# Attention: exponentials turned by products with diagonal matrices of the reciprocal sums, in place of scaling them and transposing

## The chip, the cores and the metric

The kernel runs on one core of a Trainium2 chip. The metric is the device time of one execution in microseconds (us); the median of the runs of the kernel before is 1780.18 us. Five engines work side by side, each with its own list of instructions, and meet through semaphores: PE (TensorE, matrix products; PEld is its loading of weights), DVE (VectorE), ACT (ScalarE), POOL (GpSimd) and SP (which issues the DMAs of this kernel).

## The reference, cut to what matters

The network is a block with gated linear attention and an MLP, then a block with a gated delta rule, a sparse attention and an MLP, on 512 tokens of width 1024 in float32. The change is in the sparse attention, whose last lines are

```python
s = jnp.einsum('bqcgd,bqncd->bqcgn', qg, k_g).astype(jnp.float32) * scale
s = jnp.where(valid[:, :, None, None, :], s, -jnp.inf)
p = jax.nn.softmax(s, axis=-1).astype(v_g.dtype)
o = jnp.einsum('bqcgn,bqncd->bqcgd', p, v_g)
```

There are 8 query heads, 2 key heads, and head size 128. The softmax needs, for each query, the exponentials of its scores divided by their sum.

## The kernel before, in words

The attention (lines 1371 to 1497) works through 8 steps, i = 0 to 7, one query head each, with e = i % 2 the key head and the parity of most buffers. A step handles all 512 queries in 4 tiles q of 128; tile q has P * (q + 1) keys, so the scores of a head are 128 x 1280 numbers, kept in `ms[e]` with queries on partitions. In the order of the data, a step is:

- `queries` (L1446, DVE) scales the head's queries; `turn` (L1131, PE) multiplies them by a swap matrix; `pool_rope` (L1136, POOL) and `dve_rope` (L1142 and L1145, DVE) make the rotated queries `aq`.
- `scores` on PE (L1395) makes 4 products of 512, 384, 256 and 128 columns.
- `scores` on DVE (L1461) adds the mask, takes the maximum and writes `ms[e]`; L1466 scales the maxima.
- ACT takes the exponential in place (L1433) with the sums in `r_sum`.
- DVE inverts the sums (L1471) and scales the 4 tiles of `ms[e]` in place (L1475), one `tensor_scalar` each.
- PE transposes the 10 blocks of 128 x 128 that are on or below the diagonal into PSUM (L1409), in the order of `K_ORDER`; the counter `pt_ps` rises three times in a step.
- ACT copies them to `p_t` (L1438, four copies). PE multiplies them with the values (L1416, four products, 1280 columns in all). DVE multiplies by the gate (L1454).

The engines run these in an order written by hand (`body`). In body i, PE does the scores of step i + 1, the transposes of step i, the products with the values of step i, then `turn` of step i + 2. DVE does the reciprocal and the scaling of step i, the masks of step i + 1, `queries` of step i + 2, `output` of step i, then the rope of step i + 2. ACT does the exponentials and the copies of step i. The last body has no work ahead in it. Each engine takes its list strictly in that order. After the attention a fence lets all engines meet, and the gated delta rule follows.

Of the kernel before, what the change touches and what calls it, by code (L numbers as in the profile page):

```python
# [19 lines left out]
ALU = mybir.AluOpType  # L20
# [3 lines left out]
P = 128  # L24
SEQ, D, DFF = 512, 1024, 4096
KT = D // P
TT = SEQ // P
# [72 lines left out]
def build(nc, t, out, const_square, const_wide, gb_rows):  # L100
    with ExitStack() as ctx:
        def sb(name, shape, dt=F32):
            return ctx.enter_context(nc.sbuf_tensor(name, shape, dt))
# [4 lines left out]
        s = {}  # L108
# [19 lines left out]
        ident = sb("ident", [P, P])  # L128
# [10 lines left out]
        def take(*shape):  # L139

            n = int(np.prod(shape))
            v = arena[:, at[0]:at[0] + n]
            at[0] += n
            assert at[0] <= 22400, at[0]
            if len(shape) == 2:
                v = v.rearrange("p (a b) -> p a b", a=shape[0])
            if len(shape) == 3:
                v = v.rearrange("p (a b c) -> p a b c", a=shape[0], b=shape[1])
            return v
# [4 lines left out]
        def tiles(ap, n=TT):  # L154
            return ap.rearrange("p (t c) -> p t c", t=n)
# [902 lines left out]
        ms = [None, ci_si_keep[:, 0:1280]]  # L1058
# [16 lines left out]
        n_max, r_sum = take(2 * TT), take(TT)  # L1075
# [4 lines left out]
        av = take(2, SEQ)  # L1080
        gtmp = take(3, SEQ)
        lg = gtmp[:, 0:2]
        top8 = take(3, 8)
        assert at[0] <= kept0, (at[0], kept0)
        off = [0, 128, 384, 768]
# [41 lines left out]
        def pe_rope(pe, c, src, swap):  # L1127

            if not (isinstance(c, int) and c == 0):
                pe.wait_ge(s["rp_ss"], c)  # L1130
            pe.matmul(b[5][:], swap[:], src, start=True, stop=True).then_inc(s["rp_ps"], 1)  # L1131
# [6 lines left out]
        def dve_rope(dve, c, src, sin):  # L1138
            if not (isinstance(c, int) and c == 0):
                dve.wait_ge(s["rp_out"], c)  # L1140
            dve.wait_ge(s["rp_ps"], c + 1)
            dve.tensor_tensor(rp_s, b[5][:], sin, ALU.mult).then_inc(s["rp_ss"], 1)  # L1142
            dve.wait_ge(s["rp_cc"], c + 1)
            dve.wait_ge(s["rp_ss"], c + 1)
            dve.tensor_tensor(src, rp_c, rp_s, ALU.add).then_inc(s["rp_out"], 1)  # L1145
# [226 lines left out]
        S_ORDER = (3, 1, 0, 2)  # L1372
# [4 lines left out]
        def att_steps(eng, body):  # L1377

            with eng.Fori(0, HPK - 1) as j:
                body(j, 0, 2)  # L1380
                body(j, 1, 2)
            body(HPK - 1, 0, 1)
            body(HPK - 1, 1, 0)

        def pe_att(pe):
            def turn(i, e):

                pe.wait_ge(s["r_y"], i + 3)
                pe_rope(pe, i + 7, aq[:, e], swap_a)

            def scores(i, e):
                pe.wait_ge(s["rp_out"], i + 8)
                for q in S_ORDER:
                    bk, o = s_at[q]
                    last = pe.matmul(bk[:, o:o + P * (q + 1)], aq[:, e, q * P:(q + 1) * P], ak[:, e, 0:P * (q + 1)],  # L1395
                                     start=True, stop=True)
                    if q != 0:
                        last.then_inc(s["s_ps"], 1)

            def body(j, e, ahead):  # L1400
                i = 2 * j + e
                if ahead >= 1:
                    pe.wait_ge(s["nm_r"], TT * i + TT)
                    scores(i + 1, 1 - e)
                pe.wait_ge(s["pn_r"], TT * i + TT)
                for k in K_ORDER:
                    bk, o = t_at[k]
                    for q in range(k, TT):
                        last = pe.transpose(bk[:, o + (q - k) * P:o + (q - k + 1) * P],  # L1409
                                            ms[e][:, off[q] + k * P:off[q] + (k + 1) * P], ident[:])  # L1410
                    if k != 3:
                        last.then_inc(s["pt_ps"], 1)
                pe.wait_ge(s["att_done"], i + 1)
                for n, k in enumerate(K_ORDER):
                    pe.wait_ge(s["pt_sb"], TT * i + n + 1)
                    last = pe.matmul(b[4][:, k * P:SEQ], v_key[e][:, k, :], p_t[:, koff[k]:koff[k] + SEQ - k * P],  # L1416
                                     start=(n == 0), stop=(n == TT - 1), skip_group_check=True)
                last.then_inc(s["pv_ps"], 1)
                if ahead >= 2:
                    turn(i + 2, e)  # L1420

            turn(0, 0)
            scores(0, 0)
            turn(1, 1)
            att_steps(pe, body)

        def act_att(act):
# [14 lines left out]
        def dve_att(dve):  # L1442
            def queries(j, e):
                i, h = 2 * j + e, j + HPK * e
                dve.wait_ge(s["r_r"], h + 3)
                dve.scalar_tensor_tensor(aq[:, e], q_all[:, bass.ds(h, 1)].rearrange("p a t -> p (a t)"),  # L1446
                                         gains[:, G_QN:G_QN + 1], q_sq[:, bass.ds(h, 1)].rearrange("p a t -> p (a t)"),
                                         ALU.mult, ALU.mult).then_inc(s["r_y"], 1)

            def output(j, e):  # L1450
                i, h = 2 * j + e, j + HPK * e
                dve.wait_ge(s["pv_ps"], i + 1)
                o = o_att[:, bass.ds(h, 1)].rearrange("p a t -> p (a t)")
                dve.scalar_tensor_tensor(o, o, 1.0, b[4][:], ALU.add, ALU.mult).then_inc(s["att_done"], 1)  # L1454

            def scores(i, e):
                for n, q in enumerate(S_ORDER):
                    dve.wait_ge(s["s_ps"], (TT - 1) * i + (1, 2, 3, 3)[n])
                    w = P * (q + 1)
                    bk, o = s_at[q]  # L1460
                    dve.tensor_tensor_reduce(out=ms[e][:, off[q]:off[q] + w], in0=bk[:, o:o + w], in1=sel[:, off[q]:off[q] + w],  # L1461
                                             scale=1.0, scalar=NOT_CAUSAL, op0=ALU.add, op1=ALU.max,
                                             accum_out=n_max[:, 4 * e + q:4 * e + q + 1]).then_inc(s["nm_r"], 1)
                dve.wait_ge(s["nm_r"], TT * i + TT)
                nm = n_max[:, 4 * e:4 * e + 4]
                dve.tensor_scalar(nm, nm, -P ** -0.5, None, ALU.mult).then_inc(s["nms"], 1)  # L1466

            def body(j, e, ahead):
                i = 2 * j + e
                dve.wait_ge(s["ex_a"], TT * i + TT)  # L1470
                dve.reciprocal(r_sum, r_sum).then_inc(s["rs_r"], 1)  # L1471
                dve.wait_ge(s["rs_r"], i + 1)
                for q in S_ORDER:
                    m = ms[e][:, off[q]:off[q] + P * (q + 1)]
                    dve.tensor_scalar(m, m, r_sum[:, q:q + 1], None, ALU.mult).then_inc(s["pn_r"], 1)  # L1475
                if ahead >= 1:
                    scores(i + 1, 1 - e)
                if ahead >= 2:
                    queries(j + 1, e)
                output(j, e)  # L1480
                if ahead >= 2:
                    dve_rope(dve, i + 9, aq[:, e], sa)

            queries(0, 0)
            dve_rope(dve, 7, aq[:, 0], sa)
            queries(0, 1)
            scores(0, 0)
            dve_rope(dve, 8, aq[:, 1], sa)
            for i in range(ATT_H):
                body(i // 2, i % 2, min(2, ATT_H - 1 - i))  # L1490
# [739 lines left out]
```

## Time and profile before

| | us |
|---|---|
| median of 3 runs | 1780.18 |
| lowest, highest | 1779.96, 1781.19 |
| the profiled execution | 1785.38 |
| its span in the trace | 1783.6 |
| of which the attention, from its first `queries` to its last `output` | 872.8 to 948.9 |

The profiled execution took 5.2 us more than the median of the runs without a profiler, and 1.8 us of it lie outside the span. The trace tells where in the span each engine was busy (us from the span's start), what an idle engine waited for, and, in the chain, which piece of work released the next one, back from the end. The granted clock of TensorE is given as a share of full speed (2.4 GHz); 0.50 is the lower of its two levels.

### The profile page before, as it was taken

Reading aid. Unit: us, or ns where it says so; the run is one execution under the profiler, and the core shown is the slowest. Engines: PE = TensorE matmul, PEld = TensorE weight load, DVE = VectorE, ACT = ScalarE, POOL = GpSimd, SP = SyncE. Lnnn points to the kernel's source line nnn. Section 1 sums busy time; section 2 is a strip of 40 time slices with the busy share of each in tenths; the row PEclk is TensorE's granted clock in tenths of the full one; section 3 lists DMA queues with packets and bytes.
Section 4 is the critical chain, followed back from the end, with each engine's and each line's share of the span. In section 5 each row is a group of like instructions: output and inputs, shape, how many; then the busy total and the mean of one; then the engine's idle time right before and its main releaser. Section 6 shows DMA issues by size and latency. Waiting matters only on the chain.

```text
span 1783.6 us, 24801 instructions
## 1 busy us (share of the span) xinstructions
PE 1659.3 (93%) x9418; PEld 1316.4 (74%) x9418; DVE 984.9 (55%) x1489; ACT 680.3 (38%) x1033; POOL 241.9 (14%) x220
## 2 busy tenths in 40 slices
PE   6899968999999987899879898998989899999999
PEld 4677757888888864567547786877878688888887
DVE  5455545444454455378775757566674544444453
ACT  6355543313132334223444535254443332313232
POOL 0134330000000030134210311304022000000000
PEclk7999979999999997899999999999999999999999
DMA  4222202333333332223102213121220233333333
GB/s 136 72 60 72 71 13 82 95 96 93 105 94 94 94 87 73 59 60 83 50 0 83 60 49 83 39 70 49 72 70 15 82 86 103 94 95 94 106 93 96
DMA packets 258157, 135.06 MB, mean 76 GB/s; under 512 B 10699, under 2 KB 254940, under 8 KB 258068
## 3 DMA queue, kind: packets, MB, share of 16 engines
q1 hardware_dynamic: 258068, 133.84, 26.6%
q8 instruction: 61, 1.00, 0.2%
q14 instruction: 28, 0.23, 0.0%
HBM read 131.64 MB, written 2.18 MB: 75 GB/s over the span
## 4 chain that ended last, share of the span: by engine, by line
PE 70%; DVE 11%; issue 10%; ACT 6%; POOL 3%; DMA 0%; DVEq 0%; POOLq 0%; PEldq 0%; ACTq 0%; SPq 0%; PEld 0%
PE bank L229 17%; PE bank L230 17%; PE bank L231 17%; PE bank L1574 3%; DVE arena L1880 3%; PE bank L491 2%; DVE w_lo L213 2%; ACT w_hi L209 2%; PE bank L493 1%; PE bank L492 1%; PE bank L1395 1%; PE bank L1416 1%; PE bank L1131 1%; PE bank L1590 1%; PE bank L1627 1%
## 5 line engine op out<-in xcount | busy, mean ns | idle before, releaser
L229 PE MATMUL bank<-h_hi,w_hi 128*128 128x512 f32 x984 | 401.7, 408 | 38.4 <-DVEq L1899 13.7
L230 PE MATMUL bank<-h_lo,w_hi 128*128 128x512 f32 x984 | 391.3, 398 | 0.0
L231 PE MATMUL bank<-h_hi,w_lo 128*128 128x512 f32 x984 | 390.9, 397 | 0.0
L213 DVE TENSOR_TENSOR w_lo<-raw,w_hi 128x1024 fp32r<-128x1024 f32 x218 | 281.2, 1290 | 141.3 <-ACT w_hi L209 139.4
L209 ACT CAST w_hi<-raw 128x1024 fp32r<-128x1024 f32 x234 | 245.1, 1047 | 254.5 <-PE bank L231 243.1
L229 PEld LDWEIGHTS bank<-h_hi,w_hi 128*128 128x128 f32 x984 | 189.8, 193 | 97.0 <-issue 36.7
L229 PE MATMUL bank<-m_hi,w_hi 128*128 128x512 f32 x608 | 238.7, 393 | 6.4 <-DVE w_lo L213 6.2
L231 PE MATMUL bank<-m_hi,w_lo 128*128 128x512 f32 x608 | 237.3, 390 | 0.0
L230 PE MATMUL bank<-m_lo,w_hi 128*128 128x512 f32 x608 | 237.2, 390 | 0.0
L230 PEld LDWEIGHTS bank<-h_lo,w_hi 128*128 128x128 f32 x984 | 190.6, 194 | 41.3 <-issue 3.2
L231 PEld LDWEIGHTS bank<-h_hi,w_lo 128*128 128x128 f32 x984 | 189.7, 193 | 41.0
L229 PEld LDWEIGHTS bank<-m_hi,w_hi 128*128 128x128 f32 x608 | 114.4, 188 | 33.2 <-issue 6.5
L231 PEld LDWEIGHTS bank<-m_hi,w_lo 128*128 128x128 f32 x608 | 114.5, 188 | 24.1
L230 PEld LDWEIGHTS bank<-m_lo,w_hi 128*128 128x128 f32 x608 | 114.6, 188 | 23.4
L948 DVE TENSOR_TENSOR arena<-bank,arena 128x512 f32<-128x512 f32 x64 | 44.3, 692 | 147.0 <-PE bank L231 147.0
L938 DVE TENSOR_TENSOR arena<-arena 128x512 f32<-128x512 f32 x64 | 44.3, 693 | 133.4 <-ACT arena L914 133.4
L491 PE MATMUL bank<-h_hi,w_hi 128*128 128x512 f32 x248 | 106.2, 428 | 0.0
L914 ACT ACTIVATE arena<-bank 128x512 f32<-128x512 f32 x64 | 38.3, 598 | 175.4 <-PE bank L231 175.4
L493 PE MATMUL bank<-h_hi,w_lo 128*128 128x512 f32 x248 | 97.2, 392 | 0.0
L492 PE MATMUL bank<-h_lo,w_hi 128*128 128x512 f32 x248 | 96.9, 391 | 0.0
L1574 PE MATMUL bank<-arena 64*64 64x64 f32 x1984 | 73.0, 220 | 7.1 <-DVE arena L2022 4.0
L1574 PEld LDWEIGHTS bank<-arena 64*64 64x64 f32 x1984 | 67.2, 134 | 13.2 <-issue 10.5
(273 smaller groups left out, 2027.9 us busy)
## 6 DMA issues: line engine op xcount, KB each, us to landing
raw<-in_l_w_ff SPq DMA_DIRECT2D x64, 512.0 KB, 4.0
raw<-in_w_in SPq DMA_DIRECT2D x64, 512.0 KB, 3.8
raw<-in_w_mlp_up SPq DMA_DIRECT2D x32, 512.0 KB, 4.0
raw<-in_w_mlp_down SPq DMA_DIRECT2D x32, 512.0 KB, 3.7
raw<-in_l_w_in SPq DMA_DIRECT2D x24, 512.0 KB, 3.8
raw<-in_l_w_out SPq DMA_DIRECT2D x8, 512.0 KB, 3.7
arena<-gb_rows SPq DMA_DIRECT2D x16, 256.0 KB, 4.6
raw<-in_w_out SPq DMA_DIRECT2D x8, 512.0 KB, 3.7
```

Of the source, the lines that this page charges most:

```text
L209: act.copy(w_hi[q.par][:], raw[q.par][:]).then_inc(s["w_hi_ready"], 1)
L213: dve.tensor_tensor(w_lo[q.par][:], raw[q.par][:], w_hi[q.par][:].bitcast(F32), ALU.subtract).then_inc(s["w_ready"], 1)
L229: pe.matmul(g_bank[q.par][:], w_hi[q.par][:, k], hi[:, k], start=(k == 0), stop=False)
L230: pe.matmul(g_bank[q.par][:], w_hi[q.par][:, k], lo[:, k], start=False, stop=False)
L231: last = pe.matmul(g_bank[q.par][:], w_lo[q.par][:, k], hi[:, k], start=False, stop=(k == KT - 1))
L491: pe.matmul(g_bank[q.par][:], w_hi[q.par][:, k], hi[:, k], start=(k == 0), stop=False)
L492: pe.matmul(g_bank[q.par][:], w_hi[q.par][:, k], lo[:, k], start=False, stop=False)
L493: last = pe.matmul(g_bank[q.par][:], w_lo[q.par][:, k], hi[:, k], start=False, stop=(k == KT - 1))
L938: dve.tensor_tensor(sq[:, u % 2], rl[:, u % 2], rl[:, u % 2], ALU.mult).then_inc(s["sqr"], 1)
L948: dve.tensor_tensor(down[:, u % 2], g_bank[q.par][:], r_sqr, ALU.mult).then_inc(s["dn"], 1)
L1574: return pe.matmul(o, left, right, start=True, stop=True, skip_group_check=True)
L1880: dve.scalar_tensor_tensor(y, ub[:, jj:jj + SEQ], w, y, ALU.mult, ALU.add).then_inc(s["c_chain"] if jj < CONV - 1 else s["c_y"], 1)
```

## The change

The scaling of the 4 tiles of exponentials is gone. Instead DVE makes `r_dg`, four 128 x 128 diagonal matrices with the reciprocal sums of the four tiles of queries on their diagonals, in one `tensor_tensor`, in a part of the arena that nothing used. PE then multiplies each 128 x 128 block of unscaled exponentials with the diagonal matrix of its tile of queries, as an ordinary float32 `matmul`, where it transposed the block with the identity before. The product of a block's transpose with the diagonal matrix is the scaled and transposed block. Since `r_dg` is a single buffer, DVE waits before it writes it until the products of the step before have read it.

```diff
+        r_dg = tiles(gtmp[:, 2])
...
-                pe.wait_ge(s["pn_r"], TT * i + TT)
+                pe.wait_ge(s["pn_r"], i + 1)
                 for k in K_ORDER:
                     bk, o = t_at[k]
                     for q in range(k, TT):
-                        last = pe.transpose(bk[:, o + (q - k) * P:o + (q - k + 1) * P],
-                                            ms[e][:, off[q] + k * P:off[q] + (k + 1) * P], ident[:])
+                        last = pe.matmul(bk[:, o + (q - k) * P:o + (q - k + 1) * P],
+                                         ms[e][:, off[q] + k * P:off[q] + (k + 1) * P], r_dg[:, q], start=True, stop=True)
...
                 dve.reciprocal(r_sum, r_sum).then_inc(s["rs_r"], 1)
                 dve.wait_ge(s["rs_r"], i + 1)
-                for q in S_ORDER:
-                    m = ms[e][:, off[q]:off[q] + P * (q + 1)]
-                    dve.tensor_scalar(m, m, r_sum[:, q:q + 1], None, ALU.mult).then_inc(s["pn_r"], 1)
+                if i:
+                    dve.wait_ge(s["pt_ps"], (TT - 1) * i)
+                dve.tensor_tensor(r_dg, ident[:].unsqueeze(1).broadcast_to([P, TT, P]),
+                                  r_sum.unsqueeze(2).broadcast_to([P, TT, P]), ALU.mult).then_inc(s["pn_r"], 1)
```

## Rows read from the trace of the kernel before

**Rows 1.** Chain of work, 868 to 955 us, one step: start us, us, what

```profile
892.38 2.43 PE bank L1395 x8
894.81 1.09 PE bank L1409 x10
895.90 0.02 issue
895.92 2.43 PE bank L1416 x8
898.35 0.87 PE bank L1131 x2
...
899.31 0.70 DVE arena L1142
...
900.11 0.70 DVE arena L1145
```

**Rows 2.** Timeline, steps 2 and 6: start, us, engine, line, operation, idle time before and releaser

```profile
900.86 2.43 PE L1395 MATMUL bank<-arena 128*128 128x512 f32 x8 [1.65 <-DVE arena L1145]
900.92 1.27 DVE L1475 TENSOR_SCALAR arena<-arena 128x512 f32<-128x512 f32 x4
...
903.12 1.26 PE L1409 MATMUL bank<-ident,arena 128*128 128x128 f32 x10
...
903.75 1.42 ACT L1438 COPY arena<-bank 128x512 f32<-128x512 f32 x4 [4.89 <-PE bank L1409]
...
904.39 0.30 PEld L1416 LDWEIGHTS bank<-arena 128*128 128x128 f32 x2 [0.26 <-ACT arena L1438]
...
937.06 1.26 PE L1409 MATMUL bank<-ident,arena 128*128 128x128 f32 x10
...
941.07 0.21 ACT L1433 ACTIVATION_READ_ACCUMULATOR arena<-arena 128x1 f32 x1
```

**Rows 3.** Waits of the stretch 868 to 955 us: total us, times, longest us

```profile
PE bank L1409 <- DVE arena L1475: 2.2, 1, 2.2
```

**Rows 4.** Groups by line and shape, 872 to 951 us: count, busy us, mean ns

```profile
L1409 PE MATMUL bank<-ident,arena 128*128 128x128 f32 x80 | 11.1, 290 | 2.2 <-DVE arena L1475 2.2
...
L1145 DVE TENSOR_TENSOR arena<-arena 128x512 f32<-128x512 f32 x8 | 5.5, 692 | 0.8
...
L1438 ACT COPY arena<-bank 128x512 f32<-128x512 f32 x8 | 4.7, 586 | 34.7 <-PE bank L1409 34.7
```

**Rows 5.** Chain, 1000 to 1013 us: 16 products with 128 columns, in one run

```profile
1008.70 3.57 PE bank L1590 x32
```

**Rows 6.** Groups by line and shape of DVE, whole span

```profile
L1932 DVE TENSOR_TENSOR arena<-arena 128x512 f32<-128x512 f32 x8 | 9.8, 1227 | 0.0
```

**Rows 7.** Chain of the last step, 936 to 949 us

```profile
938.43 2.41 PE bank L1416 x8
...
940.86 0.69 DVE arena L1454
941.55 0.10 DVE arena L1471
...
941.67 1.29 DVE arena L1475 x4
...
943.01 2.31 PE bank L1409 x10
945.32 2.85 PE bank L1416 x8
```

**Rows 8.** Stretches of PE: us, length, busy (instructions), granted clock, DMA share, GB/s

```profile
942.00:943.00 1.00, 0.00 (x0) 1.00 0.00 0
943.00:944.00 1.00, 0.99 (x5) 0.57 0.00 0
...
945.00:946.00 1.00, 1.00 (x4) 0.50 0.00 0
946.00:947.00 1.00, 1.00 (x4) 0.72 0.00 0
```

**Rows 9.** Other idle times of PE and the clock in and after them

```profile
247.70:249.60 1.90, 0.08 (x1) 1.00 0.00 0
249.60:251.00 1.40, 1.34 (x9) 0.73 0.05 12
```

**Rows 10.** The same for steady steps of the attention (all engines)

```profile
892.00:901.00 9.00, 6.95 (x29) 4.24 (x30) 6.48 (x21) 3.58 (x12) 1.27 (x1) 1.00 0.00 0
901.00:910.00 9.00, 7.33 (x30) 4.38 (x31) 6.51 (x20) 3.58 (x12) 1.27 (x1) 1.00 0.00 0
```

## The prediction

> **What bounds the kernel now.** I read the chain of waits first, cut to the attention. A step of it repeats every 8.47 us, and PE carries most of it [rows 1]: the scores of the next head (2.43 us), the ten transposes (1.09), the products with the values (2.43), the product that turns the next queries (0.87); then PE stands still for 1.65 us while DVE does the two halves of the rope, and it begins again [rows 1, 2]. The reader should see what is not in this chain: neither the scaling L1475 nor the copies L1438.
>
> Then I read the timeline of step 2. The scaling runs from 900.92 to 902.19, while PE is at the scores that it began at 900.86; PE turns to the transposes at 903.12 [rows 2]. DVE is done 0.93 us before it is asked. The waits say the same for all steps: the transposes waited for the scaling once only, for 2.2 us [rows 3], and that is the last step, where no scores of a next head stand in between [rows 7]. So in seven of eight steps the work that the change takes from DVE is free, and what it adds to PE is on the path.
>
> One more thing is in the timeline. Ten transposes should need 1.09 us, but from the first of them to the first product with the values 1.27 us pass: this product waited for the first copy of ACT, which began at 903.75 and takes 0.586 us for its largest piece [rows 2, 4]. So 0.18 us of a step belong to ACT, under which longer PE work can hide.
>
> **The change, part by part.**
>
> *Transposes become products.* A transpose is one instruction of 128 columns: 80 for 8 steps of 10 [rows 4], 0.109 us apart (1.09 over 10) [rows 1]. The trace has no product with a diagonal matrix, but it has float32 products of the same size, 128 x 128 with 128 columns and new weights each time: L1590 issues 16 in a run, they show as 32 instructions, and the run takes 3.57 us, 0.112 us an instruction [rows 5]. The scores tell the same: 4 products, 8 instructions [rows 1]. So a product costs two instructions of about the same time as one transpose, 0.223 us. Ten take 2.23 us.
>
> After that the first copy is no longer late: its four blocks are 8 of the 20 instructions, done after 0.90 us; the copy begins some 0.19 us behind them (as now: four transposes are 0.44 us, and it begins 0.63 us after the first of them), takes 0.59 us, and is through at 1.7 us, before 2.23 [rows 2, 4]. A step therefore grows from 1.27 to 2.23 us between the first block and the first product with the values: +0.96 us. In step 6 the distance now is 1.37 (937.06 to 938.43) [rows 2, 7], so +0.86. Seven steps: 6 x 0.96 + 0.86 = **+6.6 us**. Bounds: if the wait of 0.18 us for a copy stays, +0.18 each, +7.9 in all; if the products go at 0.109 us as the transposes do, -0.06 each, +6.2. I take 0.112, the row of the same shape.
>
> *Scaling becomes one multiplication on DVE.* Four instructions, 1.27 us [rows 2], go; one `tensor_tensor` of 128 x 512 float32 from SBUF comes. L1145 is the same shape at 0.692 us [rows 4]; the highest row of this shape is L1932 at 1.227 us [rows 6]. The operands here are read with repeats, which no row of L1145 has; I take 0.69 and keep 1.23 as the upper end. At either, DVE stays ahead of PE in steps 0 to 6, so the worth is nothing; even at 1.27 us it was 0.93 early. What starts earlier behind it on DVE are the masks L1461, and these wait for PE's scores. In the last step it is on the path: 1.29 - 0.69 = **-0.6 us** [rows 7] (bounds -0.1 to -0.6). From this I take 0.1 back: the last two copies of step 6 now end later than they do, since the products end later, and with them the last exponentials, which are in ACT's queue behind these copies. They end at 941.28 now, 0.27 us before the reciprocal begins [rows 2, 7], and would end about level with it. That leaves **-0.5 us**.
>
> *The new wait of DVE on `pt_ps`.* Behind it are the multiplication, the masks of the next head, `queries`, `output` and the rope, so a late answer would be dear. It is never late: on PE the products of step i - 1 come before the products with the values of step i - 1, and DVE has waited for those in `output` of step i - 1 already. Cost: the 0.02 to 0.04 us of a wait that is met, beside work of PE. Nothing on the path.
>
> *TensorE's clock in the last step.* Now PE stands still from 940.84 to 943.01, 2.17 us [rows 7], and as it starts again its granted clock falls from 1.00 to 0.57 and 0.50, that is to 1.2 GHz, until about 946.3 [rows 8]. Transposes and products take 2.31 + 2.85 = 5.16 us there [rows 7], where the transposes and products of a steady step have 1.09 + 2.43 = 3.52 [rows 1]. With the change the stop is 2.17 - 0.5 = 1.7 us. The steps before show such stops seven times between 882 and 935, of 1.65 us (the last of them 1.74), with the clock at 1.00 throughout (one stop stands in [rows 2], two of the stretches with their clock in [rows 10]); after a stop of 1.9 us at 247.7 it fell [rows 9]. 1.7 is nearer to 1.65. I take it that the clock stays: 2.23 + 2.43 = 4.66 in place of 5.16, **-0.5 us**. If it falls as now, for 3.3 us at half speed, 1.65 us are lost: 6.31 in place of 5.16, +1.15.
>
> *The sum.* +6.6 - 0.5 - 0.5 = **+5.6 us**, and everything behind the fence shifts by it: the profiled execution would go from 1785.38 to 1791.0, its span from 1783.6 to 1789.2. That execution is 5.2 us over the median; the difference is the profiler's and I carry it over. Forecast for the median: 1780.18 + 5.6 = **1785.8 us**. Its own range, from 0.109 us an instruction (-0.4) to the wait for the copy that stays (+1.3) and a multiplication of 1.23 us (+0.5): 1785.2 to 1787.6, and about 0.6 us either way for how the runs differ.
>
> **The rivals.**
>
> *The clock falls in the last step all the same.* All as above, but +1.15 in place of -0.5: +7.3 us, **1787.5**. For it speaks that stops of 1.7 and 1.9 us are near each other, and that the products will be at another place in time. Against it: seven stops of 1.65 to 1.74 us without a fall.
>
> *A product is one instruction, as a transpose is (the other side).* If a product with a diagonal matrix went through at the price of a transpose, 10 x 0.112 = 1.12 us, the copy would stay the later of the two, seven steps would not change, and the last step would gain: -0.5 for the shorter work on DVE, and 1.12 + 0.18 + 2.43 = 3.73 in place of 5.16. Together -1.9 us, **1778.3**: not slower. It decides for the change as soon as ten blocks take less than about 1.4 us. Against it: every float32 product that I looked at has two instructions [rows 1, 5].
>
> *DVE's work is on the path in every step.* If PE's stop of 1.65 us hung on how early DVE gets to the rope, the 0.6 us saved would come back seven times: 5.6 - 4.2 = +1.4 us, **1781.6**, no difference that can be measured. Against it: before the rope DVE waits for PE's turned queries, not the reverse, and before the transposes it is 0.93 us early.
>
> *A product costs four times a transpose.* Then ten take 40 x 0.109 = 4.36 us, a step grows by 3.1, and with the last step (4.36 + 2.43 for 5.16, and -0.5) the sum is 7 x 3.1 + 1.1 = +22.8 us, **1803**. Against it are the 32 instructions for 16 products [rows 5].
>
> The Trainium skill, "TensorE: Matmul & The Clock Gate", section Terms, says that the transpose mode is 4x faster for FP32, which speaks against this change and would give that last time. The trace doesn't bear it out: it has a factor of two, 0.223 us to 0.109.
>
> **How the numbers follow.** Forecast 0.62; the clock falls 0.18; one instruction a product 0.06; DVE on the path 0.05; four times 0.03; something that I don't see 0.06, split evenly between small drifts on both sides. The range is 1784.0 to 1788.8: it takes in the forecast with its bounds, the fallen clock with the wait for the copy that may stay, and leaves out the last three rivals. A measurement of this kernel can tell about 0.2% (3.6 us) from no change, so the border of slower is 1783.7 and that of faster 1776.6. Slower: 0.62 + 0.18 + 0.03 and most of what I don't see, 0.88. Same: 0.06 + 0.05 and a little less for what could go further, 0.10. Faster: 0.02.
>
> **What would show it.** In the trace of the changed kernel: 160 instructions at L1409's place, 0.112 us apart, and 2.23 us from the first of them to the first product with the values; the load of weights of that product no longer waits for a copy; a period of 9.43 us a step with the same stop of 1.65 before the scores; the new multiplication at 0.69 us, over 1 us before PE asks for it, and its wait on the counter without idle time; in the last step a stop of some 1.7 us, the clock at 1.00 after it. Wrong would be: a stop before the scores that is not 1.65, 80 or 320 instructions, or time that moved outside the stretch 873 to 955.

## The result

The changed kernel takes 1785.66 us at the median of 20 runs, the kernel before 1780.49 us at the median of 20. The ratio is 1.0026, with a 95% interval of 1.0018 to 1.0033: slower by 4.6 us (3.2 to 5.9); the medians as they stand differ by 5.2. The forecast was 1785.8 us.

The profile agrees where the change is. From the first `queries` of the attention to the end of its last `output`, called the stretch from here on, the kernel before took 76.1 us (872.76 to 948.88), the changed one takes 81.0 us (868.03 to 949.06): +4.9 us. The spans as wholes, 1783.6 and 1784.4 us, do not show this; the last experiment shows why. Each run has one trace, so what is said of the clock in a step is said of that one execution.

One step in the chain of waits of the changed kernel (start us, us, what; in it L1396 is the scores, L1410 the products that turn the blocks, L1417 the products with the values, L1132 the product for the queries):

```profile
897.80 2.43 PE bank L1396 x8
900.23 2.23 PE bank L1410 x20
902.46 2.16 PE bank L1417 x8
904.62 0.87 PE bank L1132 x2
...
905.59 0.70 DVE arena L1143
...
906.38 0.70 DVE arena L1146
```

Against [rows 1], 10 transposes in 1.09 us have become 20 instructions in 2.23 us, and the products with the values went from 2.43 to 2.16 us. The period of a step went from 8.47 to 9.33 us. The timeline of the same step shows why L1417 is shorter than L1416 was. First the row of the kernel before that follows the last one of step 2 in [rows 2], its load of weights for the second product, then the changed kernel:

```profile
904.93 0.19 PEld L1416 LDWEIGHTS bank<-arena 128*128 128x128 f32 x1 [0.24 <-ACT arena L1438]
```

```profile
900.06 2.39 PE L1410 MATMUL bank<-arena 128*128 128x128 f32 x20
...
901.15 0.86 ACT L1439 COPY arena<-bank 128x512 f32<-128x512 f32 x2 [5.16 <-PE bank L1410]
...
902.19 0.30 PEld L1417 LDWEIGHTS bank<-arena 128*128 128x128 f32 x2
902.29 2.32 PE L1417 MATMUL bank<-arena 128*128 128x512 f32 x8
902.73 0.19 PEld L1417 LDWEIGHTS bank<-arena 128*128 128x128 f32 x1 [0.24 <-issue]
```

Before, the first load waited 0.26 us for a copy of ACT [rows 2] and began together with its product, and the load for the second product waited for the next copy and began 0.54 us after the first. Here neither waits for ACT: the first begins 0.10 us ahead of its product, the one for the second product 0.44 us after that product. From the first block to the first product with the values it is 2.23 us (900.06 to 902.29).

The last step, in the chain, and the clock in it (the stretch, its length, PE busy, granted clock, DMA share, GB/s):

```profile
942.02 0.69 DVE arena L1455
...
942.92 0.70 DVE arena L1476
943.63 0.04 issue
943.67 2.50 PE bank L1410 x20
946.17 2.17 PE bank L1417 x8
```

```profile
942.00:943.00 1.00, 0.00 (x0) 1.00 0.00 0
943.00:944.00 1.00, 0.33 (x3) 1.00 0.00 0
944.00:945.00 1.00, 1.00 (x11) 1.00 0.00 0
945.00:946.00 1.00, 1.00 (x11) 1.00 0.00 0
```

PE stood still for 1.7 us (in [rows 7] 2.2), the clock stayed at 1.00 (in [rows 8] it fell), and the two groups took 4.67 us where they took 5.16.

### The profile page after: what moved, and what is told of

It reads as the page before. It is cut to its first block, busy times and chain, and to the rows that moved or that the text cites. A ratio compares the mean times of both kernels' runs of the same rounds, so it can differ in the third digit from the quotient of the medians.

```text
span 1784.4 us, 24944 instructions
## 1 busy us (share of the span) xinstructions
PE 1660.0 (93%) x9498; PEld 1321.1 (74%) x9498; DVE 980.8 (55%) x1465; ACT 681.3 (38%) x1033; POOL 241.8 (14%) x220
## 4 chain that ended last, share of the span: by engine, by line
PE 71%; DVE 11%; issue 9%; ACT 6%; POOL 2%; DMA 0%; DVEq 0%; POOLq 0%; PEldq 0%; ACTq 0%; SPq 0%; PEld 0%
PE bank L229 17%; PE bank L231 17%; PE bank L230 17%; PE bank L1576 3%; DVE arena L1882 3%; PE bank L491 2%; DVE w_lo L213 2%; ACT w_hi L209 2%; PE bank L493 2%; PE bank L492 2%; PE bank L1396 1%; PE bank L1410 1%; PE bank L1417 1%; PE bank L1132 1%; PE bank L1592 1%
```

## The experiments

Each comes from one of the two kernels by the edit shown. The stretch is read from its trace as above; the ratio is to the kernel before.

| run | step, us | stretch, us | median, us | ratio, 95% interval |
|---|---|---|---|---|
| before | 8.47 | 76.1 | 1780.49 | |
| after | 9.33 | 81.0 | 1785.66 | 1.0026, 1.0018 to 1.0033 |
| products with the identity | 9.33 | 83.4 | 1788.76 | 1.0037, 1.0023 to 1.0051 |
| transposes, no scaling | 8.47 | 74.1 | 1776.55 | 0.9976, 0.9966 to 0.9985 |
| transposes twice | 9.28 | 83.0 | 1787.63 | 1.0035, 1.0021 to 1.0049 |
| stop filled | 8.47 | 74.8 | 1776.42 | 0.9974, 0.9963 to 0.9986 |
| last multiplication longer | 9.33 | 83.3 | 1789.78 | 1.0053, 1.0033 to 1.0073 |
| the others longer | 9.33 | 81.5 | 1782.46 | 1.0013, 1.0001 to 1.0025 |
| before, other order | 7.96 | 72.8 | 1777.80 | 0.9985, 0.9975 to 0.9994 |
| after, other order | 7.41 | 69.5 | 1773.50 | 0.9966, 0.9952 to 0.9980 |
| before, queries first too | 6.51 | 64.5 | 1765.92 | 0.9914, 0.9899 to 0.9929 |
| after, queries first too | 7.41 | 69.6 | 1772.51 | 0.9954, 0.9941 to 0.9968 |
| before, both and the fill | 6.51 | 62.9 | 1767.80 | 0.9925, 0.9911 to 0.9938 |
| before again | 8.47 | 76.1 | 1780.99 | 0.9999, 0.9990 to 1.0008 |

**The two parts alone.** First the products without the shorter work on DVE:

```diff
-                        last = pe.transpose(bk[...], ms[e][...], ident[:])
+                        last = pe.matmul(bk[...], ms[e][...], ident[:], start=True, stop=True)
```

> One part alone: the blocks are turned by float32 products with the identity, the scaling on DVE stays as before. The stretch from the first queries to the last output of the attention was 76.1 us before and 81.0 after the change. Theory (PE's instructions set the step, DVE's scaling is hidden in seven of eight steps): steps of 9.33 us as after the change, a stop of about 2.2 us before the last products as before it, so the clock falls there (1.65 us more): stretch 83.3 us. Rival (what DVE does sets the step): the stretch stays near 76 us. If the clock held in spite of the stop: 81.7 us.

Measured: steps of 9.33 us and a stretch of 83.4 us. Then the shorter work on DVE with the transposes, from the changed kernel:

```diff
-                        last = pe.matmul(bk[...], ms[e][...], r_dg[:, q], start=True, stop=True)
+                        last = pe.transpose(bk[...], ms[e][...], ident[:])
```

> The other part alone: DVE makes the diagonal matrices in place of scaling, PE transposes with the identity as before. The kernel leaves out the division by the sums in the attention. Theory: steps of 8.47 us as before (the shorter DVE work brings nothing in them), in the last step a stop of 1.6 us in place of 2.2 and the clock at full speed after it: stretch 74.1 us against 76.1. Rival (DVE on the path in every step): 0.6 us less in each of seven steps, about 70 us. If the clock falls in the last step all the same: 75.5 us.

Measured: steps of 8.47 us and 74.1 us. So the products cost their 0.86 us in every step, and DVE's part is worth nothing in the steps but 2.0 us at the end, of which 0.6 us is its own shorter work and 1.3 us the clock: transposes and products take 3.83 us there, from 937.78 to 941.61 in the second fence below, where they took 5.16. Both came out as the theory had them. The two do not add up to the change (+7.3 - 2.0 = +5.3 against +4.9), mostly since the products alone lose more to the clock: 6.32 us where the changed kernel takes 4.67 without a fall, 1.65 us against 1.33. The last steps of the two, in the chain, first the products with the identity, then the transposes:

```profile
944.07 1.29 DVE arena L1475 x4
...
945.40 3.68 PE bank L1409 x20
949.08 2.64 PE bank L1416 x8
```

```profile
937.03 0.70 DVE arena L1476
...
937.78 1.31 PE bank L1410 x10
939.20 2.41 PE bank L1417 x8
```

**Is it the number of instructions?**

```diff
+                        for _ in range(2):
                             last = pe.transpose(bk[...], ms[e][...], ident[:])
```

> The kernel before, with every block transposed twice into the same place: as many PE instructions in a step (20) as the products have, none of them a product. Theory (the number of 128-column instructions is the price): 20 x 0.109 us = 2.18, steps of 9.3 us, in the last step the clock falls as before: stretch 82.7 us. Rival (a float32 product has a price beyond its two instructions, in its weight loads for one): steps clearly shorter than the 9.33 us of the changed kernel.

Measured: steps of 9.28 us, 0.05 less than with products, which is 20 instructions at 0.109 in place of 0.112. One step and the last one in the chain:

```profile
928.67 2.18 PE bank L1410 x20
930.86 2.16 PE bank L1417 x8
...
944.63 3.27 PE bank L1410 x20
947.90 2.99 PE bank L1417 x8
```

A float32 product of 128 columns costs what its two instructions cost. And here too L1417 takes 2.16 us and not 2.43: whatever work stands between the first block and the products with the values, ACT's copies get their time from it.

**The clock in the last step.** Two products of 512 columns that nothing reads fill PE's stop in the kernel before:

```diff
                 last.then_inc(s["pv_ps"], 1)
+                if ahead == 1:
+                    pe.wait_ge(s["nm_r"], TT * ATT_H)
+                    for _ in range(2):
+                        pe.matmul(b[0][:], aq[:, e, 0:P], ak[:, e, :], start=True, stop=True)
```

> The kernel before, with two more products of 512 columns (four instructions, some 0.9 us) that nothing reads, on PE in its stop of 2.2 us ahead of the last step's transposes; the stop that is left is 1.3 us. Theory (the length of the stop makes the clock fall): the clock stays at 1.00, the last transposes and products take 3.7 us in place of 5.16, stretch 74.6 us against 76.1. Rival (it falls for where in time it stands, or since transposes follow): no change, 76.1 us.

Measured: 74.8 us. The timeline of PE, with the fill in the second line, and the clock after it:

```profile
932.33 2.40 PE L1416 MATMUL bank<-arena 128*128 128x512 f32 x8
934.56 1.88 PE L1422 MATMUL bank<-arena 128*128 128x512 f32 x4
936.91 1.31 PE L1409 MATMUL bank<-ident,arena 128*128 128x128 f32 x10 [0.46 <-DVE arena L1479]
```

```profile
937.00:938.00 1.00, 1.00 (x10) 1.00 0.00 0
```

The fill took about 1.9 us and left a stop of 0.5 us, not the 1.3 expected (1.88 us for four instructions where I had counted 0.9), and the clock stayed. The reverse, in the changed kernel:

```diff
+                for n in range(1 if i == ATT_H - 1 else 0):
+                    dve.tensor_tensor(tiles(sc[:, SEQ * n:SEQ * (n + 1)]), ident[:]..., r_sum..., ALU.mult)
                 dve.tensor_tensor(r_dg, ident[:]..., r_sum..., ALU.mult).then_inc(s["pn_r"], 1)
```

> The changed kernel, with one more multiplication of the same shape (0.69 us, into a buffer that nothing reads) ahead of the one of the last step alone. The stop of PE before the last products becomes 1.68 + 0.69 = 2.37 us. Theory (a stop above some 1.9 us lets the clock fall): stretch 81.0 + 0.69 + 1.65 = 83.4 us. Rival (the products, unlike transposes, keep or at once regain the clock): 81.7 us.

Measured: 83.3 us; the stop was 2.3 us, and the clock fell although the work after it was products:

```profile
948.00:949.00 1.00, 0.47 (x4) 1.00 0.00 0
949.00:950.00 1.00, 1.00 (x9) 0.71 0.00 0
950.00:951.00 1.00, 1.00 (x7) 0.50 0.00 0
```

Here the clock fell 0.9 us after PE had begun again, in the kernel before after 0.1 us. So in the last step the clock follows the stop, in both kernels: seven traces have a stop of 0.5 to 1.7 us there and keep the clock, seven have one of 2.2 to 2.3 us and lose it. The fill is also work, and both edits move the time at which PE begins again, so the length is not shown to act alone. It doesn't decide elsewhere. All 14 traces have the code ahead of the attention in common, with a stop of 1.89 us near 250 us (the one of [rows 9]) and one of 2.34 us near 80 us. After the first the clock fell in 3 traces, after the second in 7. The kernel before against itself, which comes last below, has after its stop of 1.89 us

```profile
248.40:249.80 1.40, 1.36 (x12) 1.00 0.05 12
```

where [rows 9] has 0.73, and after the stop of 2.34 us the kernel with the filled stop and the one with the products with the identity have

```profile
81.50:84.50 3.00, 2.98 (x17) 1.00 0.00 0
81.70:84.70 3.00, 3.00 (x14) 0.70 0.00 0
```

What a fall costs in the last step is seen against the same work without one: 1.3 us for the transposes (5.16 against 3.83), 1.6 to 1.7 us for the products (6.32 and 6.31 against 4.67). The doubled transposes have no such partner. Against a steady step they lose as much as the products with the identity (6.26 against 4.34, 6.32 against 4.39), and in both the lower level lasted 3.4 us. The Trainium skill, "TensorE: Matmul & The Clock Gate", section Part 4: PE-mode transpose, says that transposes do not count as activity for the clock as products do; these runs give no sign of it. They are no test of it either, since in each the products with the values follow before the clock is back.

**How much DVE has to spare.**

```diff
+                for n in range(2 if i < ATT_H - 1 else 0):
+                    dve.tensor_tensor(tiles(sc[:, SEQ * n:SEQ * (n + 1)]), ident[:]..., r_sum..., ALU.mult)
```

> The changed kernel, with two more multiplications of the same shape (1.38 us of DVE, into buffers that nothing reads) in each step but the last. Theory (DVE has about 1.5 us to spare before PE asks for the diagonal matrices): steps of 9.33 us as without them, stretch 81.0 us. Rival (DVE on the path in every step): 1.38 us more in each of seven steps, 90.7 us.

Measured: steps of 9.33 us but for the first, which went to 9.78; 81.5 us. In the first step the scores of the head before had run at the lower clock and the exponentials were late, so DVE had less to spare there and PE waited. In the others 1.3 us more on DVE cost nothing. The ratio, 1.0013, is under that of the changed kernel itself, though the stretch is 0.5 us longer: a warning of how far whole times go astray here.

**Another order.** What the change gives DVE would be worth something if DVE set the step. This order makes it so. On PE, `turn` comes ahead of the products with the values; on DVE, the rope comes ahead of `output`:

```diff
+                if ahead >= 2:
+                    turn(i + 2, e)
                 pe.wait_ge(s["att_done"], i + 1)
...
                 last.then_inc(s["pv_ps"], 1)
-                if ahead >= 2:
-                    turn(i + 2, e)
...
-                output(j, e)
                 if ahead >= 2:
                     dve_rope(dve, i + 9, aq[:, e], sa)
+                output(j, e)
```

> The kernel before with another order: PE turns the queries of step i + 2 ahead of the products with the values of step i, and DVE does their rope ahead of the output of step i, so that PE's stop of 1.65 us should be filled. With it DVE becomes the longest in a step: output, reciprocal, scaling (1.27 us), masks and queries in a row before PE's turning product. Theory: steps of about 8.2 us against 8.47, stretch 74.5 us. Rival (PE's instructions alone set the step): 6.8 us a step, 66 us.

> The changed kernel with the same other order. Theory: where DVE's row of work sets the step, the shorter work of the change is worth its 0.6 us, and the longer products of PE are hidden behind DVE: steps of about 7.6 us, less than in the kernel before with this order (8.2), stretch 70.5 us. Rival (PE's instructions set the step in any order, the change costs its 0.85 us): the steps are longer than those of the kernel before with this order.

Measured: 7.96 us a step for the kernel before, 7.41 for the changed one. The chain of the first goes through DVE:

```profile
897.25 2.17 PE bank L1418 x8
...
899.45 0.69 DVE arena L1454
900.14 0.10 DVE arena L1471
...
900.26 1.28 DVE arena L1475 x4
901.54 1.65 DVE arena L1461 x8
...
903.38 0.66 DVE arena L1446
...
904.09 1.13 PE bank L1131 x2
```

The chain of the changed kernel in this order is PE alone, without a stop, so DVE no longer sets its step as the expectation had it:

```profile
896.92 2.23 PE bank L1410 x20
899.16 0.86 PE bank L1132 x2
900.02 2.16 PE bank L1419 x8
902.17 2.16 PE bank L1396 x8
```

The same change that costs 0.86 us a step in the old order brings 0.55 us in this one. I had both steps 0.2 us too long (8.2 and 7.6), in the second since I counted the scores and the products with the values at 2.26 us each where they take 2.16 without a stop or a wait.

**The queries ahead of the masks.** In the chain of the kernel before in this order, PE waits through DVE's masks L1461 for `queries` L1446, which does not need them:

```diff
+                if ahead >= 2:
+                    queries(j + 1, e)
                 if ahead >= 1:
                     scores(i + 1, 1 - e)
-                if ahead >= 2:
-                    queries(j + 1, e)
```

> The kernel before in the other order (PE turns the next queries ahead of the products with the values, DVE does the rope ahead of the output), and DVE also does the queries of step i + 2 ahead of the masks of step i + 1. DVE's masks (1.65 us) then lie beside PE's work, and neither engine waits long for the other. Theory: steps of 6.6 to 6.8 us against 7.96 with the queries behind the masks, stretch about 65 us. Rival (DVE's sum of work, scaling among it, holds the step at 7.4 or more): 69 us.

> The changed kernel in that order too. Its PE was busy without a stop in steps of 7.41 us, so moving DVE's work cannot help. Theory: steps of 7.41 us again, stretch 69.5 us; the change costs 0.7 us a step against the kernel before in this order. Rival (the shorter DVE work of the change is worth something in this order too): shorter steps than that kernel's.

Measured: 6.51 us a step for the kernel before, 7.41 for the changed one. PE is the chain in both, and the change costs 0.90 us a step again (0.7 expected; the kernel before came out under the 6.6 to 6.8 expected). One step of the kernel before in this order, and its engines' busy times in it (PE, PEld, DVE, ACT, POOL, then the clock):

```profile
899.92 1.31 PE bank L1409 x10
901.23 0.86 PE bank L1131 x2
902.09 2.16 PE bank L1418 x8
904.25 2.16 PE bank L1395 x8
```

```profile
899.90:906.40 6.50, 6.48 (x28) 4.07 (x28) 5.81 (x19) 3.70 (x12) 1.28 (x1) 1.00 0.00 0
```

This version beats both kernels: 0.9914 of the time before, 0.9899 to 0.9929. The last run adds the fill to it.

> The kernel before in that order, with the two filling products in PE's stop ahead of the last step's transposes. Theory: as with the queries first, less the 1.3 to 1.5 us that the full clock gives in the last step, stretch about 64 us, and the shortest time of all these kernels, about 1768 us. Rival: the stop in this order is another one, and the clock holds or falls whatever fills it: as without the fill.

Measured: the stretch is 62.9 us, 1.7 less, and the clock stays at the end. The median is 1767.8 us, 1.9 above that without the fill; the two intervals overlap (0.9911 to 0.9938 and 0.9899 to 0.9929). That the fill pays is seen in the stretch only.

**The kernel before against itself.**

> The kernel before, unchanged, compared with itself. In the traces so far the attention's stretch came out to 0.3 us as expected, while what lies outside it, the same code in all kernels, took anything from 1699 to 1707 us. Theory (executions of one program differ there, by where the clock of TensorE falls): the stretch is 76.1 us again, the rest is clearly off the 1707.5 us of the first profile of this kernel, and the ratio to itself is 1.000 within 0.0015. Rival (the time outside the attention belongs to the program, so that each kernel has its own): rest within 1 us of 1707.5.

Measured: the stretch 76.1 us again, the ratio 0.9999. The rest of the span is 1704.6 us, where the first profile of the same kernel has 1707.5: 2.9 us between two executions of one program. Of this nearly all lies between 230 and 270 us, in the first mixer. The same stretch of PE in the first profile and in this one:

```profile
226.00:260.00 34.00, 25.69 (x180) 0.80 0.06 16
```

```profile
226.00:260.00 34.00, 23.69 (x183) 0.86 0.06 16
```

TensorE's clock was at its lower level for longer in the one than in the other: until 236.6 us and again from 250.2 to 253.7 in the first, after the stop of 1.89 us, but only until 233.7 in this one. Over all traces the time outside the stretch, the same code everywhere, is 1699.2 to 1707.5 us; the highest two, of before and of the version with both and the fill, are those with the lowest mean clock, 0.963 both. Why the clock falls at one stop in one execution and not at the same stop in the next stays open.

## Why the prediction was right

- *PE's instructions set the step, the scaling is hidden.* Shown: the products alone give the longer step, the shorter DVE work alone gives no shorter one.
- *A product is two instructions of 0.112 us.* 160 instructions, 2.23 us for 20: as said. The Trainium skill, "TensorE: Matmul & The Clock Gate", section Terms, says that the transpose mode is 4x faster for FP32; these traces do not agree, 0.223 us against 0.109 is 2.05 times.
- *+0.96 us a step.* Mis-sized: it is +0.86. The distance to the first product with the values grew by 0.96 as worked out, but I took it that L1416 lasts 2.26 us from its start to that of `turn` in both kernels. It went from 2.26 (895.92 to 898.18) to 2.17 (902.29 to 904.46), as the load of weights for the second product no longer waits for its copy either. Seven times 0.10 is the 0.7 us between the +5.6 forecast and the +4.9 of the stretch.
- *DVE in the last step, -0.5.* The multiplication took 0.69 us as L1145 does, and the repeated operands cost nothing. The stop was 1.68 us where 1.7 was forecast. The 0.1 us taken back for the late exponentials is there too: the reciprocal has 0.19 us in the chain where it had 0.10.
- *The clock stays, -0.5.* It did, and filling or lengthening the stop moved it both ways; after a last stop of 1.69 us it stayed in all four traces that have one. Two sizes in this term were off and cancel: 2.23 + 2.43 was forecast, 2.50 + 2.17 measured. The rival's +1.65 us is what the longer last multiplication showed. What spoke for that rival, the fall after 1.9 us at 247.7, is weaker than it looked: it came in 3 of 14 traces.
- *The new wait costs nothing.* In the list of waits of the changed kernel no wait of L1476 stands. It was not taken out alone.
- *The profiled execution.* Wrong: I put the 5.2 us between the profiled execution and the median down to the profiler and forecast a span of 1789.2 us; it was 1784.4. Of the 13 later profiled executions nine lie among the other runs of their kernel, three above and one below, all at their span and 1.7 to 1.9 us. The first profile was of a long execution, above the highest of the 20 other runs (1783.55). The forecast of the median did not hang on it, since only the difference was carried over.

The lower end of the prediction's own range was added wrongly: 1780.18 + 5.6 - 0.4 is 1785.4, not 1785.2.

That 1785.8 met 1785.66 so closely is partly luck: the stretch gives +4.9 and the ratio +4.6 with 1.3 us either way.

## What to carry to other kernels

Before work is moved from one engine to another, see in the chain which of the two the step waits for: here 0.6 us taken from DVE was worth nothing and 1.1 us given to PE cost 0.86, and with two calls in another order the same edit gained 0.55 us, until a third call was moved and it cost 0.90 again. The chain also names the better edit: PE's stop of 1.65 us for a dependent pair of DVE operations was about twice what the change cost a step, and filling it by order alone, with some short waits that went too, took 1.96 us off a step and 11.6 us off the stretch. Work that is lengthened first uses up the short waits beside it (0.18 and 0.10 us here), so a row's busy time put in place of another's overstates the cost a little.

## What the runs showed of the hardware that I had not expected

A stop of PE of 1.65 to 1.74 us never lowered the granted clock in the attention's steps from the second on, one of 2.2 to 2.3 us in the last step always did (six kernels: before, products with the identity, transposes twice, the last multiplication longer, before in the other order, with the queries first too). A fall there cost 1.3 to 1.7 us against the same work without it. Ahead of the attention a stop is no such sign: after the same one of 2.34 us the clock fell in 7 of 14 traces, after the one of 1.89 us in 3. Two executions of one program can differ by 2.9 us in code that no edit touched, by the clock alone as far as the rows show; for effects of a few us the stretch around the change tells more than the span.
